# First tile's attention scores one level later in the inverse, and the first retrieval head's scores directly behind their query

## The chip, the cores and the metric

The kernel runs on one core of one Trainium2 chip. The metric is device time in microseconds (us), median of several executions. The engines are TensorE (PE; PEld is its weight load), VectorE (DVE), ScalarE (ACT), GpSimd (POOL) and SyncE (SP, which here only issues DMAs). Each engine runs its own instructions in the order they are written; the engines meet only through semaphores.

## What is computed

One residual block on 1024 tokens of width 1024. A token mixer joins gated DeltaNet (4 heads) and a sliding-window attention with sinks (8 heads); then a product-key retrieval picks 16 of 16384 experts in each of 8 heads, whose outputs are summed. Cut to what matters here:

```python
# DeltaNet, by chunks of 64 tokens: a unit lower triangular system per head
sol = lax.linalg.triangular_solve(a_mat, rhs, left_side=True, lower=True, unit_diagonal=True)
# sliding-window attention
s = jnp.einsum('bnqhgd,bnkhd->bnhgqk', qc, kb) * D ** -0.5
m = jnp.maximum(jnp.max(s, -1, keepdims=True), sink)
p = jnp.exp(s - m)
p = p / (jnp.sum(p, -1, keepdims=True) + jnp.exp(sink - m))
# retrieval
q = (xt @ wq).astype(f32).reshape(n_tok, PEER_HEADS, 2, PEER_HALF)
s1 = jnp.einsum('thd,hnd->thn', q[:, :, 0], k1.astype(f32))
s2 = jnp.einsum('thd,hnd->thn', q[:, :, 1], k2.astype(f32))
t1, i1 = lax.top_k(s1, PEER_TOPK)
t2, i2 = lax.top_k(s2, PEER_TOPK)
h = jnp.einsum('td,ted->te', xb.astype(f32), u[eb].astype(f32))   # experts' hidden values
```

## The kernel before

The program is a row of stages. `project` (to about 285 us) makes the projections. `mix_tokens` then goes through 8 tiles of 128 tokens, one after another; tile 0 takes from about 285 to 344 us. `retrieve` (about 665 to 1000 us) makes queries, scores and searches for 8 heads, and `build_gates` and `experts` follow behind a barrier. The order on every engine is written out by hand in the functions `body` (one copy per engine, run once per tile) and in the lists at the end of `tensor`, `scalar` and `vector` of `retrieve`.

**Tile 0.** The triangular inverse is found in a loop over n from 0 to 5 (`LV` is 6), whose passes are called levels here; levels 0 to 4 do the same thing in turn, level 5 a shorter form of it. At each level PE multiplies (L783), DVE masks the product (L1084, into `m_xc`), PE multiplies twice more (L804, L814), and DVE adds the results (L1093, L1101, into `m_tu`). In between, DVE carries other work: the scores of half the attention heads are scaled and masked (`softmax_scores`, L1045), their row maximum is taken (`softmax_max`, L1053 to L1058), ACT takes the exponentials (`exps`, L908 and L911), DVE sums and inverts (`softmax_sum`, L1064 and L1066), and ACT scales the probabilities (`scale_probs`, L916). DVE's `ahead` (L1013 to L1032) prepares the next tile; its step 1 (L1018) reads `m_rowB`, which a DMA brings. Only in tile 0, the output weights `w_out` are also split into two parts: SP loads them in 8 pieces into two buffers (L649), ACT rounds a piece (`split_wout`, L930), and DVE forms the remainder (`split_wout`, L1070). These lines tie the three together:

```python
            for k in range(KC):                    # SP, sync()
                if k >= 2:
                    sp.wait_ge(wout_lo, k - 1)
                sp.dma_start(wout_raw[k % 2][:], io["w_out"][k * P:(k + 1) * P, :]).then_inc(wout_in[k % 2], 16)
```

So piece k is loaded when DVE has done piece k - 2. ACT's order in tile 0 is: `exps` of the first half, piece 0, two exponentials for the next tile, `scale_probs`, pieces 1 and 2, probabilities out of PSUM, pieces 3 and 4, `exps` of the second half, pieces 5, 6 and 7, and then the copy of `uu` (L953), for which PE waits at L838. DVE does piece n - 1 at the end of level n, piece 5 behind the levels, pieces 6 and 7 later.

The tile's data come by five DMAs on SP in the order queries, keys (`m_kw`), values, gates and mask (`m_wm`); their semaphores are `tile_in[0][0]` to `tile_in[0][4]`. The keys and values of the DeltaNet for tile 0 came earlier with another semaphore. Before the change, PE waits for `tile_in[0][0]` ahead of its first transposes (L759, L761), and DVE waits for `tile_in[0][4]` ahead of everything in the tile.

**Retrieval, head 0.** The head's two queries (`query(0, 0)` and `query(0, 1)`, L1313 to L1315) are made in two halves of 512 tokens, the second of which is 24 matmuls 128x512. ACT copies each half out of PSUM (`query_half`, L1442), PE makes the scores (`score_half`, L1353), ACT copies these (`scores_half`, L1447), and DVE searches them (`search`, L1500 on). PE also makes the hidden values of a block of experts (`hidden(0, 0)` and `hidden(0, 1)`, L1326 to L1328, 12 matmuls each). Before the change each half of `hidden` stands between a query and its score. Head 1's queries follow, without a half of `hidden` between them. ACT copies head 1's queries, rounds weights (`weights`, L1392), and rounds the expert block (`split_u`, L1397); DVE waits for that at its own `split_u` (L1494), halfway through its work on head 0.

## Time and profile before

| | us |
|---|---|
| median of 3 runs | 3067.59 |
| lowest and highest | 3065.72, 3067.85 |
| profiled execution | 3062.79 |
| its span | 3061.1 |
| outside the span | 1.7 |

Shares of the span: PE 85%, PEld 66%, DVE 75%, ACT 34%, POOL 53%. The timeline gives an instruction's start and its length, and in brackets how long the engine sat idle before it and what ended the wait. An engine's next instruction can start slightly ahead of the end of the one before, since they overlap in its pipeline; distances from start to start are therefore used for work in a row.

### The profile page before, as it was taken

How to read it: one execution, taken by the hardware profiler on the slowest of the kernel's cores; microseconds unless marked ns; L12 is line 12 of the kernel's file. 1: busy time of each engine (PE TensorE's matmuls, PEld its weight loads, DVE VectorE, ACT ScalarE, POOL GpSimd, SP SyncE). 2: the span in 40 equal slices, each digit the busy share in tenths (PEclk: the TensorE clock that was granted, in tenths of full speed). 3: DMA queues.
4: the chain of work that ended last, by engine and by line, in shares of the span. 5: the costliest groups of instructions: out<-in, count | busy, mean ns of one | idle time of the engine just before them, and what ended most of it. 6: DMA issues, size and time to landing. Idle time of an engine off the chain costs nothing.

```text
span 3061.1 us, 40460 instructions
## 1 busy us (share of the span) xinstructions
PE 2617.2 (85%) x14808; PEld 2033.3 (66%) x14808; DVE 2307.9 (75%) x4894; ACT 1049.6 (34%) x1649; POOL 1620.0 (53%) x1187
## 2 busy tenths in 40 slices
PE   7998788889996565644678999999999999999996
PEld 5886676778775565542445767777767777677775
DVE  4512667657999899965777778777778777789999
ACT  4412334333544676751112222322222322222322
POOL 0010011024887555545666666677666767766774
PEclk9999899999998787876889999999999999999999
DMA  4323222131111799999999999999999999999995
GB/s 129 127 81 118 85 87 87 45 119 52 58 59 36 260 300 309 322 296 373 379 383 387 391 386 382 401 394 397 387 394 376 408 404 409 391 382 347 366 377 209
DMA packets 309808, 833.44 MB, mean 272 GB/s; under 512 B 26128, under 2 KB 114640, under 8 KB 309616
## 3 DMA queue, kind: packets, MB, share of 16 engines
q0 software_dynamic: 150864, 548.60, 46.7%
q1 hardware_dynamic: 158752, 282.31, 26.1%
q8 instruction: 116, 1.90, 0.3%
q14 instruction: 76, 0.62, 0.1%
HBM read 771.93 MB, written 58.88 MB: 271 GB/s over the span
## 4 chain that ended last, share of the span: by engine, by line
PE 18%; DVE 12%; DMA 12%; POOL 8%; issue 5%; ACT 0%; SPq 0%; DVEq 0%; ACTq 0%; POOLq 0%
DMA e_u_row<-in_u,ids 11%; POOL hold L2081 5%; DVE e_u_row L2319 3%; PE psum L2157 3%; PE psum L2124 3%; PE psum L2158 3%; PE psum L2159 3%; PE psum L2125 3%; PE psum L2126 2%; PE psum L2172 2%; POOL e_u_row L2072 2%; DVE e_y L2309 2%; DVE e_u_row L2328 1%; DVE e_vl L2277 1%; DVE hold L2328 1%
## 5 line engine op out<-in xcount | busy, mean ns | idle before, releaser
L2072 POOL DMA_INDIRECT e_u_row<-in_u,ids x384 | 485.6, 1265 | 330.3 <-DVE ids L2319 236.3
L2319 DVE CUSTOM_DVE_ANT_0 e_u_row<-e_u_row,hold 128x1024 f32<-128x1024 f32 x384 | 468.3, 1224 | 242.6 <-DMA e_u_row<-in_u,ids 242.0
L2157 PE MATMUL psum<-e_vh,e_ah 128*128 128x512 f32 x1024 | 420.7, 411 | 102.1 <-DVE e_y L2309 82.6
L2081 POOL DMA_INDIRECT hold<-in_v,ids x376 | 435.5, 1158 | 134.4 <-issue 108.8
L2158 PE MATMUL psum<-e_vl,e_ah 128*128 128x512 f32 x1024 | 409.2, 400 | 0.0
L2159 PE MATMUL psum<-e_vh,e_al 128*128 128x512 f32 x1024 | 407.4, 398 | 0.0
L2124 PE MATMUL psum<-x1d,e_uh 128*128 128x512 f32 x864 | 341.0, 395 | 0.0
L2125 PE MATMUL psum<-x1d,e_uh 128*128 128x512 f32 x864 | 337.2, 390 | 0.0
L2157 PEld LDWEIGHTS psum<-e_vh,e_ah 128*128 128x128 f32 x1024 | 198.1, 193 | 209.2 <-DVE e_y L2309 109.9
L2126 PE MATMUL psum<-x1d,e_ul 128*128 128x512 f32 x864 | 336.3, 389 | 0.0
L2309 DVE TENSOR_TENSOR e_y<-e_y,psum 128x512 f32<-128x512 f32 x464 | 299.7, 681 | 13.1 <-PE psum L2159 13.1
L1751 PE MATMUL psum<-g_one,g_two 128*128 128x128 f32 x1024 | 172.8, 348 | 130.5 <-DVE g_one L1804 130.5
L1822 POOL DMA_INDIRECT hold<-in_u,ids x128 | 191.4, 1496 | 167.1 <-DVE ids L1783 132.1
L1751 PEld LDWEIGHTS psum<-g_one,g_two 128*128 128x128 f32 x1024 | 167.7, 261 | 143.3 <-issue 143.3
L2217 ACT ACTIVATE e_a<-psum 128x512 f32<-128x512 f32 x108 | 64.3, 596 | 573.4 <-PE psum L2126 573.3
L2206 ACT ACTIVATE e_vh<-e_vr 128x1024 fp32r<-128x1024 f32 x128 | 135.4, 1058 | 339.5 <-DMA e_vr<-in_v 339.2
L2159 PEld LDWEIGHTS psum<-e_vh,e_al 128*128 128x128 f32 x1024 | 197.7, 193 | 44.0
L2158 PEld LDWEIGHTS psum<-e_vl,e_ah 128*128 128x128 f32 x1024 | 198.4, 194 | 39.0
L2172 PE MATMUL psum<-hold,e_column 128*32 128x512 f32 x1536 | 190.4, 615 | 31.4 <-ACT e_column L2223 24.2
L2124 PEld LDWEIGHTS psum<-x1d,e_uh 128*128 128x128 f32 x864 | 162.1, 188 | 64.3 <-issue 31.0
L1178 POOL TENSOR_TENSOR hold<-hold,m_lng 128x1024 f32<-128x1024 f32 x8 | 18.9, 2363 | 346.8 <-DVE hold L1001 346.8
L2212 ACT ACTIVATE e_ah<-e_a 128x512 fp32r<-128x512 f32 x128 | 81.0, 632 | 316.1 <-DVE e_a L2289 316.1
(407 smaller groups left out, 5628.9 us busy)
## 6 DMA issues: line engine op xcount, KB each, us to landing
e_vr<-in_v SPq DMA_DIRECT2D x128, 512.0 KB, 6.7
e_ur<-in_uT SPq DMA_DIRECT2D x108, 512.0 KB, 7.2
s_G<-g_tile SPq DMA_DIRECT2D x8, 4096.0 KB, 27.0
e_g<-s_G SPq DMA_DIRECT2D x64, 512.0 KB, 9.0
ids<-in_w_ch SPq DMA_DIRECT2D x17, 512.0 KB, 4.1
s_ch<-p_out POOLq DMA_DIRECT2D x16, 512.0 KB, 3.3
hold<-in_wq SPq DMA_DIRECT2D x16, 512.0 KB, 4.4
hold<-in_v,ids POOLq DMA_INDIRECT x476, 8.7
```

The lines of the kernel that those rows point to most:

```text
L1751: last = nc.tensor.matmul(psum[:, n // 4, (n % 4) * NK:(n % 4 + 1) * NK], one2[s][:, n, :], one1[s][:, n, :], start=True, stop=True)
L2072: pool.indirect_dma_start(out=u_ring[n % U_RING][:], out_offset=None, in_=io["u"], in_offset=bass.IndirectOffsetOnAxis(ap=id_u[:, s, k:k + ...
L2081: pool.indirect_dma_start(out=v_ring[m % V_RING], out_offset=None, in_=io["v"], in_offset=bass.IndirectOffsetOnAxis(ap=id_v[:, t:t + 1], a ...
L2124: nc.tensor.matmul(psum[:, j, :], uh[j][:, k, :], x1d[0][:, k, :], start=(k == 0), stop=False)
L2125: nc.tensor.matmul(psum[:, j, :], uh[j][:, k, :], x1d[1][:, k, :], start=False, stop=False)
L2126: last = nc.tensor.matmul(psum[:, j, :], ul[j][:, k, :], x1d[0][:, k, :], start=False, stop=(k == KC - 1))
L2157: nc.tensor.matmul(acc, ah[s][j][:, r], vh[s][j][:, c], start=(first and j == 0), stop=False)
L2158: nc.tensor.matmul(acc, ah[s][j][:, r], vl[s][j][:, c], start=False, stop=False)
L2159: last = nc.tensor.matmul(acc, al[s][j][:, r], vh[s][j][:, c], start=False, stop=(final and j == 1))
L2172: last = nc.tensor.matmul(psum[32 * j:32 * j + 32, 6 + c, :], column[:, 32 * (4 * (n % Z_RING) + j) + 31 - i:32 * (4 * (n % Z_RING) + j) + ...
L2309: add = nc.vector.tensor_tensor(y[:, t, c], y[:, t, c], psum[:, bank(g, q), :], ALU.add)
L2319: nc.vector.tensor_tensor_reduce(row, row, xs[:, s, :], 1.0, 0.0, ALU.mult, ALU.add, hs[:, s, k:k + 1]).then_inc(dotted, 1)
```

## The change

In tile 0 only (`before` is false there), PE no longer waits for the queries' load ahead of its transposes. The first half's attention scores (`scores(s, 0)` on PE) come behind the multiply of level 1 with their own wait for queries and keys. On DVE, `softmax_scores` and `softmax_max` of that half come at the end of level 1, and `softmax_sum` at the end of level 2 in place of level 1. DVE's wait for the mask stands behind the two products `kd` and `vb` and ahead of level 0. ACT's order in tile 0 is the same. Tiles 1 to 7 keep their order. In head 0 of the retrieval, each `score_half` of the second token half directly follows its query, and both halves of `hidden` follow the second score; on ACT, `scores_half(0, 1)` goes ahead of the first weights of head 1.

```diff
--- before.py
+++ after.py
@@ -754,17 +754,17 @@
             def body(c, i, s, before, after):
                 now = c + 1
 
-                pe.wait_ge(tile_in[s][0], 16 * (i + 1))
+                if before:
+                    pe.wait_ge(tile_in[s][0], 16 * (i + 1))
                 for h in range(GH):
                     nc.tensor.transpose(bank(2)[:, h, :], ch[s][:, GH + h, :], ident)
                 for h in range(GH):
                     last = nc.tensor.transpose(bank(3)[:, h, :], ch[s][:, 2 * GH + h, :], ident)
                 last.then_inc(S["tr"], 1)
-                pe.wait_ge(tile_in[s][1], 16 * (i + 1))
                 if before:
+                    pe.wait_ge(tile_in[s][1], 16 * (i + 1))
                     pe.wait_ge(S["ma_lo"], c)
-                scores(s, 0)
-                if before:
+                    scores(s, 0)
                     pe.wait_ge(S["mg_lo"], c)
                     pe.wait_ge(wout_lo, KC)
                     pe.wait_ge(S["h1"], 2 * (c - 1))
@@ -785,6 +785,10 @@
                     last.then_inc(lx, 1)
                     if before:
                         project_out(1 - s, sum(share[:n]), share[n])
+                    if n == 1 and not before:
+                        for part in range(2):
+                            pe.wait_ge(tile_in[s][part], 16 * (i + 1))
+                        scores(s, 0)
                     if n == 3:
                         pe.wait_ge(S["p_nrm"], 2 * c + 1)
                         transpose_probs(0)
@@ -1072,11 +1076,12 @@
 
             def body(c, i, s, before, after):
                 now = c + 1
-                dve.wait_ge(tile_in[s][4], 16 * (i + 1))
                 dve.wait_ge(S["tr"], now)
                 nc.vector.tensor_tensor(kd[:], bank(2), per_head("kdec", c), ALU.mult)
                 nc.vector.tensor_tensor(vb[:], bank(3), per_head("beta", c), ALU.mult).then_inc(S["kd"], 1)
-                softmax_scores(c, s, 0)
+                dve.wait_ge(tile_in[s][4], 16 * (i + 1))
+                if before:
+                    softmax_scores(c, s, 0)
                 for n in range(LV):
                     dve.wait_ge(lx, c * LV + n + 1)
                     if n < LV - 1:
@@ -1105,13 +1110,15 @@
                         last.then_inc(lb, 1)
                     else:
                         nc.vector.tensor_copy(full_u[blocks[0], :, blocks[1]], half_bank(3)[blocks[0]]).then_inc(lb, 1)
-                    if n == 0:
+                    if n == 1 and not before:
+                        softmax_scores(c, s, 0)
+                    if n == (0 if before else 1):
                         softmax_max(c, 0)
                     if n == 4:
                         softmax_scores(c, s, 1)
                     if after and n in (0, 1, 2, 4):
                         ahead(c + 1, i + s, 1 - s, {0: 1, 1: 2, 2: 4, 4: 5}[n])
-                    if n == 1:
+                    if n == (1 if before else 2):
                         softmax_sum(c, 0)
                     if not before and n:
                         split_wout(n - 1)
@@ -1368,11 +1375,11 @@
             score_half(1, 0)
             pe.wait_ge(mixer.x_lo, NT)
             query(0, 0, (1,))
-            hidden(0, 0)
             score_half(0, 1)
             query(0, 1, (1,))
-            hidden(0, 1)
             score_half(1, 1)
+            for part in range(2):
+                hidden(0, part)
             for h in range(1, PH):
                 query(h, 0)
                 query(h, 1)
@@ -1458,8 +1465,8 @@
             mixer.x1_high(act, 7)
             scores_half(1, 0)
             query_half(0, 1)
+            scores_half(0, 1)
             weights(1, (0,))
-            scores_half(0, 1)
             query_half(1, 1)
             scores_half(1, 1)
             weights(1, (1,))
```

DVE in tile 0, from level 1's mask. In the kernel before (`m_xc` is the masked product, `m_tu` the two running sums, `m_mx` the softmax's row values, `x1d<-hold,x1s` is a piece of `w_out`):

```order
L1084 TENSOR_TENSOR m_xc<-psum,mats 128x256
L1093 TENSOR_TENSOR m_tu<-m_tu,psum 128x256
L1101 TENSOR_TENSOR m_tu<-m_tu,psum 128x256
L1020 TENSOR_TENSOR hold<-m_rowB,hold 128x512
L1064 TENSOR_TENSOR m_mx<-m_mx 128x4
L1066 RECIPROCAL m_mx<-m_mx 128x4
L1070 TENSOR_TENSOR x1d<-hold,x1s 128x1024
L1084 TENSOR_TENSOR m_xc<-psum,mats 128x256
L1025 TENSOR_TENSOR m_qd<-m_ch,hold 128x512
```

With the change (line numbers are 4 or 5 higher):

```order
L1089 TENSOR_TENSOR m_xc<-psum,mats 128x256
L1098 TENSOR_TENSOR m_tu<-m_tu,psum 128x256
L1106 TENSOR_TENSOR m_tu<-m_tu,psum 128x256
L1049 SCALAR_TENSOR_TENSOR hold<-psum,m_wm 128x1024
L1057 TENSOR_REDUCE m_mx<-hold 128x4
L1059 TENSOR_TENSOR m_mx<-m_mx,sinks 128x4
L1061 TENSOR_TENSOR m_mx<-sinks,m_mx 128x4
L1062 TENSOR_SCALAR m_mx<-m_mx 128x4
L1024 TENSOR_TENSOR hold<-m_rowB,hold 128x512
L1074 TENSOR_TENSOR x1d<-hold,x1s 128x1024
L1089 TENSOR_TENSOR m_xc<-psum,mats 128x256
L1029 TENSOR_TENSOR m_qd<-m_ch,hold 128x512
```

The mask of the scores, the maximum and its three small operations moved from level 0 to behind level 1, ahead of the first piece of `w_out`; the sum and the reciprocal moved out, to the next level:

```order
L1098 TENSOR_TENSOR m_tu<-m_tu,psum 128x256
L1106 TENSOR_TENSOR m_tu<-m_tu,psum 128x256
L1033 TENSOR_TENSOR m_aq<-psum,hold 128x512
L1068 TENSOR_TENSOR m_mx<-m_mx 128x4
L1070 RECIPROCAL m_mx<-m_mx 128x4
L1074 TENSOR_TENSOR x1d<-hold,x1s 128x1024
```

There the sum and the reciprocal now stand directly ahead of the second piece of `w_out`.

PE in the retrieval's head 0, at the end of the second half of the first query, before:

```order
L1314 MATMUL psum<-x1d,w 128x512
L1315 MATMUL psum<-x1d,w 128x512
L1326 MATMUL psum<-x1d,r_uh 128x512
L1327 MATMUL psum<-x1d,r_uh 128x512
L1328 MATMUL psum<-x1d,r_ul 128x512
```

and with the change:

```order
L1321 MATMUL psum<-x1d,w 128x512
L1322 MATMUL psum<-x1d,w 128x512
L1360 MATMUL psum<-r_kk,hold 128x128 x4
L1320 MATMUL psum<-x1d,r_wh 128x512
L1321 MATMUL psum<-x1d,r_wh 128x512
```

The scores (`r_kk`) moved up to the query; 12 matmuls of `hidden` went from here to behind the second score.

ACT there, before:

```order
L1442 ACTIVATE hold<-psum 128x512
L1392 ACTIVATE w<-hold 128x1024
L1447 ACTIVATE r_sc<-psum 128x512
L1442 ACTIVATE hold<-psum 128x512
L1447 ACTIVATE r_sc<-psum 128x512
```

and with the change:

```order
L1449 ACTIVATE hold<-psum 128x512
L1454 ACTIVATE r_sc<-psum 128x512
L1399 ACTIVATE w<-hold 128x1024
L1449 ACTIVATE hold<-psum 128x512
L1454 ACTIVATE r_sc<-psum 128x512
```

The copy of the scores (`r_sc`) moved ahead of the rounding of the weights.

## Rows read from the trace of the kernel before

**Rows 1.** The page's first line: span and instructions of the whole execution.
```profile
span 3061.1 us, 40460 instructions
```

**Rows 2.** Timeline of DVE, tile 0: start, length, instruction, [idle before <-releaser].
```profile
293.66 0.69 DVE L1077 TENSOR_TENSOR m_kd<-psum,d_kdec 128x512 f32<-128x512 f32 x1 [9.09 <-DMA m_wm<-in_wmask]
...
294.87 1.22 DVE L1045 SCALAR_TENSOR_TENSOR hold<-psum,m_wm 128x1024 f32<-128x1024 f32 x1
...
296.00 0.41 DVE L1084 TENSOR_TENSOR m_xc<-psum,mats 128x256 f32<-128x256 f32 x1
...
298.00 1.21 DVE L1053 TENSOR_REDUCE m_mx<-hold 128x4 f32<-128x1024 f32 x1
...
300.76 0.69 DVE L1018 TENSOR_TENSOR hold<-m_rowB,hold 128x512 f32<-128x512 f32 x1 [1.07 <-DMA m_rowB<-s_rows]
```

**Rows 3.** Timeline of DVE, tile 0, inverse levels 1 to 3 and later.
```profile
303.86 0.42 DVE L1101 TENSOR_TENSOR m_tu<-m_tu,psum 128x256 f32<-128x256 f32 x1 [0.43 <-PE psum L814]
...
304.80 0.16 DVE L1064 TENSOR_TENSOR m_mx<-m_mx 128x4 f32<-128x4 f32 x1
...
306.20 0.42 DVE L1084 TENSOR_TENSOR m_xc<-psum,mats 128x256 f32<-128x256 f32 x1
...
308.80 1.22 DVE L1070 TENSOR_TENSOR x1d<-hold,x1s 128x1024 fp32r<-128x1024 f32 x1
...
309.94 0.42 DVE L1084 TENSOR_TENSOR m_xc<-psum,mats 128x256 f32<-128x256 f32 x1
...
325.30 1.20 DVE L1070 TENSOR_TENSOR x1d<-hold,x1s 128x1024 fp32r<-128x1024 f32 x1
```

**Rows 4.** Timeline of ACT, tile 0, same columns.
```profile
299.72 0.51 ACT L908 ACTIVATE hold<-hold,m_mx 128x256 f32<-128x256 f32 x1 [13.98 <-DVE m_mx L1058]
...
301.70 0.19 ACT L911 ACTIVATE m_mx<-m_mx 128x4 f32<-128x4 f32 x1
...
305.88 1.69 ACT L916 ACTIVATE hold<-hold,m_mx 128x256 f32<-128x256 f32 x4
...
331.73 1.06 ACT L930 ACTIVATE x1s<-hold 128x1024 fp32r<-128x1024 f32 x1 [2.53 <-DMA hold<-in_w_out]
...
332.70 0.58 ACT L953 ACTIVATE m_uu<-psum 128x512 f32<-128x512 f32 x1
```

**Rows 5.** DMA issues, 255 to 345 us: count, KB, median us to landing.
```profile
hold<-in_w_out SPq DMA_DIRECT2D x8, 512.0 KB, 4.0
```

**Rows 6.** Timeline of PE, tile 0, same columns.
```profile
301.84 1.12 PE L804 MATMUL psum<-m_xc,m_tu 64*64 64x64 f32 x16 [3.49 <-DVE m_xc L1084]
...
306.67 0.68 PE L804 MATMUL psum<-m_xc,m_tu 64*64 64x64 f32 x16 [0.73 <-DVE m_xc L1084]
...
333.33 2.08 PE L838 MATMUL psum<-m_uu,m_kd 128*128 128x128 f32 x8 [5.05 <-ACT m_uu L953]
```

**Rows 7.** Timeline of PE, retrieval's head 0.
```profile
694.46 0.39 PE L1326 MATMUL psum<-x1d,r_uh 128*128 128x512 f32 x1
...
697.18 1.05 PE L1353 MATMUL psum<-r_kk,hold 128*128 128x128 f32 x8
...
707.05 0.48 PE L1313 MATMUL psum<-x1s,w 128*128 128x512 f32 x1
```

**Rows 8.** Timeline of ACT, retrieval's heads 0 and 1.
```profile
694.66 0.60 ACT L1442 ACTIVATE hold<-psum 128x512 f32<-128x512 f32 x1 [6.54 <-PE psum L1315]
...
731.93 1.04 ACT L1397 ACTIVATE r_uh<-r_ur 128x1024 fp32r<-128x1024 f32 x1
```

**Rows 9.** Timeline of DVE, retrieval's heads 0 and 1.
```profile
699.01 0.87 DVE L1500 MAX8 r_top<-r_sc 128x8 f32<-128x128 f32 x4 [5.00 <-ACT r_sc L1447]
...
708.07 0.87 DVE L1500 MAX8 r_top<-r_sc 128x8 f32<-128x128 f32 x4 [3.80 <-ACT r_sc L1447]
...
733.00 1.60 DVE L1494 TENSOR_TENSOR r_ul<-r_ur,r_uh 128x1024 fp32r<-128x1024 f32 x1 [7.43 <-ACT r_uh L1397]
```

**Rows 10.** Windows, 734 to 1000 us: busy PE, PEld, DVE, ACT, POOL; PEclk, DMA, GB/s.
```profile
734.00:1000.00 266.00, 225.94 (x1035) 187.51 (x1033) 253.68 (x1504) 127.45 (x108) 211.38 (x96) 0.92 0.16 51
```

## Prediction, made before the changed kernel ran

> **What bounds the kernel now.** I read three views: the timelines of the first tile engine by engine, the timelines around the retrieval's head 0, and one window over the rest of the retrieval. The shares of the page don't help, since the two edited places are 60 us and 40 us of a span of 3061.1 us [rows 1], each with a limit of its own. The stages follow each other with nothing to fill a gap, so I carry a delay of either place to the end in full.
>
> Tile 0 begins with DVE idle until the mask lands at 293.66, and later it stands still once more until `m_rowB` lands at 300.76 [rows 2]. Its end is set by ACT: the copy of `uu` at 332.70 is queued behind the last piece of `w_out`, which ACT could start only when it had landed at 331.73 [rows 4], and PE waited 5.05 us for `uu` [rows 6]. That last piece was sent for when DVE had done piece 5, begun at 325.30 and ended at 326.50 [rows 3], so it took 5.2 us to land, where the median of the eight is 4.0 [rows 5]. The path through tile 0 is thus DVE's row of levels and pieces, one load, and ACT.
>
> In head 0 of the retrieval DVE idles 5.00 and 3.80 us for scores, and then 7.43 us for ACT's rounding of an expert block [rows 9]. ACT does that at 731.93 [rows 8], behind the copies of head 1's queries, which PE makes from 707.05 on without a pause [rows 7]. From 734 to 1000 us DVE is busy 253.68 of 266 us [rows 10], so whatever moves the end of the third idle time moves the rest.
>
> **Start of tile 0: nothing on the path.** PE's transposes and DVE's two products go ahead of the load, and DVE's level 0 starts at 293.7, when the mask is there, instead of 296.00 [rows 2]: 2.3 us earlier. But the next-tile step with `m_rowB` still stands between level 0 and level 1, and its landing doesn't depend on DVE: SP sends for it before the first `w_out`. It starts at 300.76 as before; the idle time grows from 1.07 us by the 2.3 us and by the maximum, which is no longer there. The scores on PE lie in that hole too.
>
> **Levels 1 and 2: +5.3 us.** DVE's last addition of level 1 starts at 303.86 as before [rows 3] and the next instruction about 0.35 later, at 304.2. Now come the scores (294.87 to 296.00, 1.13 us [rows 2]): 305.3. The maximum and its small ones, which begin when the scores are written, take 1.7 us to ACT's start (298.00 to 299.72 [rows 2, 4]): 307.1. ACT's exponentials take 299.72 to 301.70 and 0.19 [rows 4], 2.2 us: 309.3. Only behind these stands ACT's piece 0 (1.06 us [rows 4]): 310.3. DVE has one small step to do meanwhile and then waits for it; its piece 0 takes 1.14 us from start to start (308.80 to 309.94 [rows 3]). Level 2 starts at 311.5 instead of 306.20. Before, the exponentials ran while DVE waited for `m_rowB`; that cover is gone.
>
> **Level 2 to level 3: +3.1 us more.** Before, DVE went from level 2's start to piece 1 in 2.60 us and finished it in 1.14 [rows 3], together 3.74, because ACT had long rounded that piece. Now the sum and the reciprocal come first (0.3 us; the sum alone is the 0.16 us row of [rows 3]), then ACT scales the probabilities (four in about 1.6 us [rows 4]), then rounds piece 1 (1.06), each handing over in some 0.05 us, and only then does DVE do its piece: 2.60 + 0.3 + 1.6 + 1.06 + 0.1 + 1.14 = 6.8. That is 3.1 more, and level 3 starts 8.4 us later than before. From there DVE has the same list as before, ACT's pieces are ahead of it, and each load follows DVE's pieces; at the median 4.0 us the loads keep up. So piece 5, the last load and `uu` are 8.4 us later.
>
> **PE's clock: +2.6 us.** After an idle time of 3.49 us the sixteen small matmuls of a level took 1.12 us, and after one of 0.73 us only 0.68 [rows 6]: 0.44 us more for L804, and the same again for L814 behind it, 0.88 us a level. That is the engine at 1.2 instead of 2.4 GHz. With the change PE stands idle about 6 us ahead of level 2 and some 2 us more twice until level 3. I charge levels 2, 3 and 4, 2.6 us, as that row after 3.49 us is the nearest; the ends are 0 (the clock stays up) and 3.5 (four levels).
>
> Tile 0 is then 5.3 + 3.1 + 2.6 = 11.0 us longer, with bounds 8.4 - 1.2 = 7.2 (the clock stays up and the last load takes 4.0 instead of 5.2) and 8.4 + 3.5 = 11.9.
>
> **Retrieval, head 0: +1.7 us.** Between a query and its score must lie ACT's copy. The query ended at 694.46, where `hidden` began; ACT started 0.20 later [rows 7, 8], and PE starts 0.63 us after ACT's start, as with `uu` (332.70 to 333.33 [rows 4, 6]). Before, 2.72 us of `hidden` (694.46 to 697.18 [rows 7]) covered that. Now PE idles 0.83 us twice, and as the same matmuls have to be done, head 1's queries start at 708.7 instead of 707.05: 1.7 us. For DVE the two searches start earlier, at 699.01 - (2.72 - 0.83) = 697.1, and at 708.07 - 3.8 = 704.3: here two halves of `hidden` are gone, 5.4 us, and two gaps have come, 1.7. But its next wait, until 733.00 [rows 9], ends with ACT's rounding of the block behind head 1's queries. It only grows from 7.43 to 7.4 + 3.8 + 1.7 = 12.9 us and ends at 734.7. ACT's and POOL's rounding of head 1's weights come later by one copy of scores, about 1.7 us, and were finished well ahead of their use. The bounds are 0 (a gap is covered somehow) and 1.7, since a gap of 0.83 us is about the 0.73 us which left the clock up in [rows 6].
>
> **Sum.** 11.0 + 1.7 = 12.7 us. The profiled execution took 3062.79 us, 1.7 outside its span, and would be 3075.5. The median of the runs is 3067.59, 4.8 above it; the same 12.7 us on it give 3080.3, and I forecast 3080.
>
> **The rivals.**
> *The slack in front of `uu` hides part of tile 0.* PE waits 5.05 us for `uu` [rows 6], so DVE's row of levels has about that much slack if the last loads don't depend on it. Then tile 0 costs 11.0 - 5.05 = 6.0, and the time is 3067.6 + 6.0 + 1.7 = 3075.3. Against it: the loads wait for DVE's pieces by the code quoted above, and all pieces shift. Chance 0.08.
>
> *The retrieval's gain gets through.* DVE is the busiest engine from 734 us on, and its search starts 3.8 us earlier. If the 7.43 us of [rows 9] ended by the DMA of the block rather than by PE's queries, DVE would keep the 3.8: 3067.6 + 11.0 - 3.8 = 3074.8. The Trainium skill (Perfetto Trace Analysis, Identifying Performance Opportunities) says to take the most contended engine of a stretch and to make what its gaps wait for start sooner, which is what this edit does for DVE; by that rule it is a gain. The row says the gap behind is the one that decides, with ACT idle until PE's queries. Chance 0.09.
>
> *Faster.* Both at once, at one point: if DVE doesn't fall behind the loads of `w_out` by more than the 5.05 us in front of `uu`, tile 0 costs nothing, and the search's 3.8 us remain: 3063.8. It decides at the second piece: were ACT to have it rounded before `scale_probs`, level 3 would be only 5.3 us late. ACT's order speaks against it. Chance 0.07.
>
> *The forecast,* with tile 0 between 7.2 and 11.9 and the retrieval between 0 and 1.7, that is 3074.8 to 3081.2 and on either side some 2 us by which the medians of different runs stand apart: chance 0.76, its own range 3073 to 3083.
>
> **How the numbers follow.** The range that holds the time 8 times in 10 runs from 3070 to 3085: the forecast's, and both partly hidden cases. A measurement of this kernel can tell about 0.2%, 6.1 us, from no change, so slower begins at 3073.7. The faster rival gives 0.07. Of the two partly hidden cases (0.17) more than half, and of the forecast's low end a little, fall below 3073.7 once the runs' own spread is added: 0.14 for no change. Slower is left with 0.79.
>
> **What would show it.** In tile 0: DVE idle some 5 us until `m_rowB`, still at about 300.8; idle about 2.5 us ahead of piece 0 and nearly 3 ahead of piece 1, both ended by ACT L930's counterpart; level 2 at 311.5; `uu` at about 344; L804's counterpart at 1.12 us in levels 2 and 3. In the retrieval, seen relative to the tile's shift: two gaps of 0.8 us on PE in front of the scores, head 1's queries 1.7 us later, DVE's wait for the block 12.9 us. I am wrong if `m_rowB` lands earlier, if DVE finds piece 0 or 1 ready, or if the stages behind take up a shift.

## The result: slower by 0.4%

| | before | after |
|---|---|---|
| median of 10 runs each | 3063.56 us | 3072.95 us |
| lowest and highest | 3057.98, 3067.85 | 3069.38, 3077.55 |
| profiled execution | 3062.79 | 3069.38 |
| its span | 3061.1 | 3067.7 |

The ratio is 1.0039, with a 95% interval of 1.0029 to 1.0050: slower by 0.4%, 11.9 us by the ratio and 9.4 by the medians. The forecast was 3080.0 with a range of 3070 to 3085. The ratio is not the quotient of the two medians, which is 1.0031. The lines of the changed kernel are numbered 4, 5 or 7 higher in the places shown.

**Tile 0.** First DVE's timeline of the changed kernel: start in us, length, engine and line, operation, output and inputs, and in brackets the idle time before it and what ended that.

```profile
294.07 0.42 DVE L1089 TENSOR_TENSOR m_xc<-psum,mats 128x256 f32<-128x256 f32 x1 [5.90 <-DMA m_wm<-in_wmask]
...
301.34 0.69 DVE L1022 TENSOR_TENSOR hold<-m_rowB,hold 128x512 f32<-128x512 f32 x1 [4.35 <-DMA m_rowB<-s_rows]
...
304.78 1.22 DVE L1049 SCALAR_TENSOR_TENSOR hold<-psum,m_wm 128x1024 f32<-128x1024 f32 x1
...
310.90 1.23 DVE L1074 TENSOR_TENSOR x1d<-hold,x1s 128x1024 fp32r<-128x1024 f32 x1 [2.59 <-ACT x1s L934]
312.04 0.42 DVE L1089 TENSOR_TENSOR m_xc<-psum,mats 128x256 f32<-128x256 f32 x1
...
318.56 1.23 DVE L1074 TENSOR_TENSOR x1d<-hold,x1s 128x1024 fp32r<-128x1024 f32 x1 [2.72 <-ACT x1s L934]
319.70 0.42 DVE L1089 TENSOR_TENSOR m_xc<-psum,mats 128x256 f32<-128x256 f32 x1
...
323.67 0.42 DVE L1089 TENSOR_TENSOR m_xc<-psum,mats 128x256 f32<-128x256 f32 x1
327.37 0.42 DVE L1098 TENSOR_TENSOR m_tu<-m_tu,psum 128x256 f32<-128x256 f32 x1 [3.29 <-PE psum L808]
...
337.56 1.19 DVE L1074 TENSOR_TENSOR x1d<-hold,x1s 128x1024 fp32r<-128x1024 f32 x1
```

Four idle times behind the start stand out. DVE is through with level 0 early and stands 4.35 us until `m_rowB` is there (1.07 us in [rows 2]). It stands 2.59 and 2.72 us for ACT's pieces 0 and 1, where it had no wait before, and it stands 3.29 us in level 4 for PE, where it was 1.61 us before. The level starts (L1089) are at 294.07, 301.95, 312.04, 319.70 and 323.67. ACT's timeline shows where pieces 0 and 1 come from:

```profile
307.75 0.51 ACT L912 ACTIVATE hold<-hold,m_mx 128x256 f32<-128x256 f32 x1 [21.56 <-DVE m_mx L1062]
...
309.83 1.04 ACT L934 ACTIVATE x1s<-hold 128x1024 fp32r<-128x1024 f32 x1
...
315.88 1.70 ACT L920 ACTIVATE hold<-hold,m_mx 128x256 f32<-128x256 f32 x4 [3.54 <-DVE m_mx L1070]
317.48 1.99 ACT L934 ACTIVATE x1s<-hold 128x1024 fp32r<-128x1024 f32 x2
...
342.57 1.06 ACT L934 ACTIVATE x1s<-hold 128x1024 fp32r<-128x1024 f32 x1 [1.69 <-DMA hold<-in_w_out]
343.53 0.58 ACT L957 ACTIVATE m_uu<-psum 128x512 f32<-128x512 f32 x1
```

ACT has done nothing for 21.56 us when the row maximum comes at 307.75. Its exponentials run until 309.7, and only behind them comes piece 0 (309.83). Piece 1 (317.48) stands behind `scale_probs` (315.88), which had to wait for DVE's reciprocal. In [rows 4] the exponentials began at 299.72, at a time when DVE was waiting for a DMA anyway. At the end the last piece (342.57) and `uu` (343.53) follow each other as in [rows 4]. PE's timeline:

```profile
294.55 1.12 PE L808 MATMUL psum<-m_xc,m_tu 64*64 64x64 f32 x16 [7.16 <-DVE m_xc L1089]
...
302.42 1.12 PE L808 MATMUL psum<-m_xc,m_tu 64*64 64x64 f32 x16 [3.19 <-DVE m_xc L1089]
...
312.51 1.12 PE L808 MATMUL psum<-m_xc,m_tu 64*64 64x64 f32 x16 [5.91 <-DVE m_xc L1089]
...
320.17 1.12 PE L808 MATMUL psum<-m_xc,m_tu 64*64 64x64 f32 x16 [1.45 <-DVE m_xc L1089]
...
322.93 2.08 PE L723 MATMUL psum<-m_kw,hold 64*128 64x256 f32 x8
...
326.64 0.68 PE L808 MATMUL psum<-m_xc,m_tu 64*64 64x64 f32 x16
...
344.16 2.07 PE L842 MATMUL psum<-m_uu,m_kd 128*128 128x128 f32 x8 [3.62 <-ACT m_uu L957]
```

L808, the counterpart of L804 in [rows 6], takes 1.12 us in levels 0 to 3 and 0.68 us in level 4. The second half's scores (L723) take 2.08 us, just behind 1.12 us ones. The longer times are PE at the lower of its two clock levels. Level 1 had 1.12 us before the change too [rows 6]; what is new is the low clock in levels 0, 2 and 3 and in the matmuls of level 4 ahead of L808. Windows of 4 us show the clock for both kernels (us, then busy us and instruction count of PE, PEld, DVE, ACT and POOL, then the granted clock as a share of 2.4 GHz, the DMA share and GB/s). Before:

```profile
304.00:308.00 4.00, 3.21 (x58) 2.76 (x56) 3.73 (x9) 3.28 (x7) 0.00 (x0) 0.87 0.18 25
308.00:312.00 4.00, 3.12 (x68) 2.68 (x70) 3.17 (x7) 2.48 (x3) 0.00 (x0) 1.00 0.54 143
312.00:316.00 4.00, 3.94 (x66) 3.24 (x62) 2.33 (x5) 1.06 (x1) 0.00 (x0) 1.00 0.58 224
...
320.00:324.00 4.00, 3.04 (x16) 2.63 (x16) 3.90 (x8) 2.37 (x10) 0.00 (x0) 0.50 0.44 139
```

and after:

```profile
304.00:308.00 4.00, 2.61 (x32) 2.30 (x28) 3.47 (x8) 0.24 (x1) 0.00 (x0) 0.78 0.01 5
308.00:312.00 4.00, 0.00 (x0) 0.00 (x0) 1.41 (x2) 4.00 (x12) 0.00 (x0) 0.65 0.00 0
312.00:316.00 4.00, 2.83 (x48) 2.64 (x48) 2.75 (x8) 0.46 (x2) 0.00 (x0) 0.50 0.35 131
...
320.00:324.00 4.00, 3.83 (x54) 3.54 (x56) 2.35 (x5) 0.91 (x2) 0.00 (x0) 0.50 0.36 131
```

From 308 to 316, levels 3 and 4 of the kernel before, the clock was 1.00; after, PE does nothing from 308 to 312, and then has 0.50, that is 1.2 GHz. Before had its own stretch at 0.50, but later, from 320 on.

To compare the stages I count from the first DVE instruction of the tile's preparation (`m_xc`, 283.69 before, 284.14 after, which is t0 below), as the stages ahead differ by 0.45 us.

| after t0, us | level 0 | 1 | 2 | 3 | 4 | `uu` |
|---|---|---|---|---|---|---|
| before | 12.31 | 17.68 | 22.51 | 26.25 | 29.39 | 49.01 |
| after | 9.93 | 17.81 | 27.90 | 35.56 | 39.53 | 59.39 |
| difference | -2.38 | +0.13 | +5.39 | +9.31 | +10.14 | +10.38 |

**Retrieval, head 0.** PE's timeline of the changed kernel:

```profile
701.77 0.39 PE L1322 MATMUL psum<-x1d,w 128*128 128x512 f32 x1
702.85 1.16 PE L1360 MATMUL psum<-r_kk,hold 128*128 128x128 f32 x8 [0.69 <-ACT hold L1449]
703.76 0.48 PE L1320 MATMUL psum<-x1d,r_wh 128*128 128x512 f32 x1
...
710.14 1.16 PE L1360 MATMUL psum<-r_kk,hold 128*128 128x128 f32 x8 [0.69 <-ACT hold L1449]
```

and DVE's, whose third row is the forming of the expert block's remainder (L1501):

```profile
704.78 0.88 DVE L1507 MAX8 r_top<-r_sc 128x8 f32<-128x128 f32 x4 [3.24 <-ACT r_sc L1454]
...
712.08 0.88 DVE L1507 MAX8 r_top<-r_sc 128x8 f32<-128x128 f32 x4 [2.02 <-ACT r_sc L1454]
...
742.45 1.61 DVE L1501 TENSOR_TENSOR r_ul<-r_ur,r_uh 128x1024 fp32r<-128x1024 f32 x1 [12.87 <-ACT r_uh L1404]
```

DVE waits 3.24 and 2.02 us for the scores where [rows 9] have 5.00 and 3.80, so the searches do start sooner. PE stands 0.69 us ahead of each score for ACT's copy of the query, where the matmul in the third row starts without a wait. And DVE's next wait, for ACT's rounding of the expert block (L1404), has grown from 7.43 us [rows 9] to 12.87. From tile 7's last layer norm to the end of that wait it is 63.41 us before and 65.31 after: 1.90 us more.

**Where the profiled execution's 6.6 us lie.** +0.45 ahead of t0, +10.38 in tile 0, -1.84 in tiles 1 to 7, -1.44 from there to the layer norm, +1.90 in head 0, +0.36 in the rest of the retrieval, and -3.21 in the gates and experts. The change reaches none of the negative places. Most of the -1.84 and the -1.44 is two stretches in which the kernel before had a low clock and the changed one did not, as the windows show. Before:

```profile
490.00:494.00 4.00, 4.00 (x25) 3.23 (x23) 1.44 (x5) 2.65 (x5) 0.00 (x0) 0.66 0.02 4
650.00:654.00 4.00, 4.00 (x11) 3.19 (x12) 0.00 (x0) 1.04 (x2) 3.92 (x3) 0.60 0.00 0
```

and after:

```profile
500.00:504.00 4.00, 3.94 (x58) 3.34 (x56) 2.30 (x7) 2.66 (x5) 0.00 (x0) 1.00 0.02 4
659.00:663.00 4.00, 4.00 (x17) 3.26 (x18) 0.00 (x0) 1.05 (x2) 3.92 (x3) 1.00 0.00 0
```

These are the same places of the same tiles, and PE is busy 3.94 to 4.00 of 4 us in all of them. The last term is the gates and experts, unchanged in every kernel here: 2058.1 us before and 2054.9 after in the profiles, and from 2051.5 to 2060.9 over the twelve profiles of this study. A run's time therefore scatters by several us whatever is done elsewhere (how the 9.4 us come about was not looked into), and the experiments below are read by stage as well as by their ratios.

### The profile page after: what moved, and what is told of

The parts are those of the page before. It is cut to its first block, busy times and chain, and to the rows that moved or that the text cites. A ratio compares the mean times of both kernels' runs of the same rounds, so it can differ in the third digit from the quotient of the medians.

```text
span 3067.7 us, 40461 instructions
## 1 busy us (share of the span) xinstructions
PE 2615.0 (85%) x14808; PEld 2031.9 (66%) x14808; DVE 2307.7 (75%) x4894; ACT 1048.1 (34%) x1649; POOL 1601.2 (52%) x1187
## 4 chain that ended last, share of the span: by engine, by line
PE 14%; DMA 13%; DVE 13%; POOL 9%; issue 6%; ACT 0%; DVEq 0%; SPq 0%; ACTq 0%; POOLq 0%
DMA e_u_row<-in_u,ids 12%; POOL hold L2088 6%; DVE e_u_row L2326 3%; POOL e_u_row L2079 3%; PE psum L2164 2%; PE psum L2131 2%; PE psum L2165 2%; PE psum L2166 2%; PE psum L2132 2%; PE psum L2133 2%; DVE e_y L2316 2%; PE psum L2179 2%; DVE e_u_row L2335 2%; DVE e_vl L2284 1%; DVE hold L2335 1%
## 5 line engine op out<-in xcount | busy, mean ns | idle before, releaser
L2088 POOL DMA_INDIRECT hold<-in_v,ids x376 | 428.0, 1138 | 130.5 <-issue 109.2
```

The lines of the kernel that those rows point to most:

```text
L2088: pool.indirect_dma_start(out=v_ring[m % V_RING], out_offset=None, in_=io["v"], in_offset=bass.IndirectOffsetOnAxis(ap=id_v[:, t:t + 1], a ...
```

## Experiments

All are timed beside runs of the kernel before on the same chip; the medians of those were 3060.67 us (e1 to e4), 3059.97 (e5 to e8) and 3058.76 (e9, e10). My theory was that tile 0 pays through ACT's order and DVE's waits plus PE's clock, and the retrieval through PE's two gaps; the rivals were that the slack ahead of `uu` hides part of it, and that DVE keeps its earlier search. Each kernel has one profile, so a stage's time is one sample. Where nothing waits for a DMA and the clock is the same, the samples repeat: levels 1 to 2, 2 to 3 and 3 to 4 take 10.10, 7.65 and 3.97 us in e1 and 10.09, 7.66 and 3.97 in the changed kernel, the same code. The loads do not: `uu` comes 49.01, 49.34 and 47.37 us after t0 in the kernel before, e2 and e7, which have the same tile 0.

### e1: the change in tile 0 alone

The changed kernel with the retrieval's order put back.

```diff
             query(0, 0, (1,))
+            hidden(0, 0)
             score_half(0, 1)
             query(0, 1, (1,))
+            hidden(0, 1)
             score_half(1, 1)
-            for part in range(2):
-                hidden(0, part)
...
+            weights(1, (0,))
             scores_half(0, 1)
-            weights(1, (0,))
```

> The change with the retrieval's part undone. My theory (nearly all of the loss is in tile 0, where ACT's exponentials and scaling now stand uncovered in front of the pieces of w_out, with PE at 1.2 GHz on top): the copy of uu 10 to 11 us later than in the kernel before, tiles 1 to 7 and the retrieval unchanged but for that shift, and 3 to 4 us of it lost or not by chance in single stretches where PE's clock drops; time 10 us over the kernel before. Rival (the first tile's loss is made up by slack in the later stages, and the retrieval is what costs): time within 3 us of the kernel before.

Measured: 3070.61 us, ratio 1.0053 [1.0037, 1.0069]. Levels 2, 3 and 4 start 27.10, 34.76 and 38.72 us after t0 and `uu` 58.15, 9.1 later than before. From the layer norm to the end of the wait for the block's rounding it is as long as before (63.44 us). So tile 0 alone makes nearly all of the loss, and no slack hides it. The run times fit that but say little on the size: the six runs give 16 us by the ratio and 9.9 by the medians, which lies below the ratio's own interval (11 to 21 us). Tile 0 lost 9.1 us to `uu` here and 10.4 in the changed kernel, with the same instructions. Of the 1.2 us, 0.8 is `m_rowB`, which let level 1 start at 17.00; from there to level 4 the steps are equal. In level 4 DVE waited 2.44 us for PE here and 3.29 there, and the last load took 0.4 us more here.

### e2: the change in the retrieval alone

The kernel before with the same lines of `tensor` and `scalar` in `retrieve` in the changed order.

```diff
             query_half(0, 1)
-            weights(1, (0,))
-            scores_half(0, 1)
+            scores_half(0, 1)
+            weights(1, (0,))
             query_half(1, 1)
```

> Only the retrieval's part of the change on the kernel before. My theory (head 1's queries decide): two gaps of 0.8 us on PE ahead of the scores, DVE's wait for the rounded expert block about 13 us instead of 7.4, and the rest of the retrieval 1.7 to 1.9 us later; time 1.7 us over the kernel before. Rival (DVE, the busiest engine there, keeps what its searches gain): DVE's work behind that wait starts 3.8 us earlier, time 3.8 us under the kernel before.

Measured: 3061.37 us, 1.0009 [0.9997, 1.0021]. PE's timeline:

```profile
694.47 1.16 PE L1353 MATMUL psum<-r_kk,hold 128*128 128x128 f32 x8 [0.69 <-ACT hold L1442]
...
701.77 1.16 PE L1353 MATMUL psum<-r_kk,hold 128*128 128x128 f32 x8 [0.69 <-ACT hold L1442]
```

and DVE's:

```profile
734.08 1.61 DVE L1494 TENSOR_TENSOR r_ul<-r_ur,r_uh 128x1024 fp32r<-128x1024 f32 x1 [12.87 <-ACT r_uh L1397]
```

The gaps of 0.69 us and the wait of 12.87 us are those of the changed kernel; from the layer norm to here it is 65.33 us where it was 63.41. The ratio can't tell +1.9 us from nothing, but it excludes the 3.8 us of gain of the second rival (0.9988), and the stage shows a loss. The Trainium skill (Perfetto Trace Analysis, Identifying Performance Opportunities) has one shorten the gaps of the most contended engine. Here two gaps of that engine were shortened, from 5.00 and 3.80 us [rows 9] to 3.23 and 2.03, and the sum with the third grew from 16.23 to 18.13 us all the same, because the third is ended by ACT behind PE's queries.

### e3: ACT rounds pieces 0 and 1 first

The changed kernel, with two pieces moved in ACT's order of tile 0.

```diff
-                exps(c, 0)
                 if not before:
                     split_wout(0)
+                exps(c, 0)
                 if after:
                     decays_ahead(act, c + 1, i + s, 1 - s)
-                scale_probs(c, 0)
                 if not before:
                     split_wout(1)
+                scale_probs(c, 0)
+                if not before:
                     split_wout(2)
```

> The changed kernel with two moves on ACT in tile 0: piece 0 of w_out is rounded ahead of the exponentials and piece 1 ahead of the scaling of the probabilities. DVE's order is as in the changed kernel. My theory (DVE's waits for pieces 0 and 1, 2.59 and 2.72 us in the changed kernel, are ACT's work put in front of them): both waits go, level 3 starts 5.3 us earlier than in the changed kernel, and as PE then idles less, up to 1 us more; time 5 to 6 us under the changed kernel, 6 us over the kernel before. Rival (the waits are for the loads of w_out): both waits stay, time as the changed kernel's.

Measured: 3069.25 us, 1.0030 [1.0016, 1.0044]. Both of DVE's waits are gone and level 3 starts at 30.28, 5.3 us earlier than in the changed kernel. At `uu` 4.5 of it are left (54.86). The run times show less than the 5 to 6 us under the changed kernel that I expected: by the ratios the two kernels are 0.1% apart, and the intervals overlap. Level 3 takes 6.16 us here for 3.97. PE waits there for the probabilities. In the changed kernel it did so as well,

```profile
317.63 1.09 PE L730 MATMUL psum<-cst,hold 128*128 128x128 f32 x8 [2.29 <-ACT hold L920]
```

but DVE was standing for piece 1 at the time. Here DVE has done piece 1 and level 3's mask, the matmuls behind the wait take 1.97 us for 1.09,

```profile
315.74 1.97 PE L730 MATMUL psum<-cst,hold 128*128 128x128 f32 x8 [2.28 <-ACT hold L920]
```

and DVE waits for what PE does behind them:

```profile
318.80 0.42 DVE L1099 TENSOR_TENSOR m_tu<-m_tu,psum 128x256 f32<-128x256 f32 x1 [3.42 <-PE psum L808]
```

So the order on ACT is one cause of the loss, but with the pieces ahead PE's wait for the probabilities, covered until then, is on the path.

### e4: filler on PE

The changed kernel with 48 more 128x128 matmuls on PE in tile 0, into a bank that nobody reads, in four groups (12, 22, 9 and 5) where PE stood idle. They add work and change no result.

```diff
                         scores(s, 0)
+                        fill(12)
...
+                    if n == 2 and not before:
+                        fill(22)
...
+                        if not before:
+                            fill(9)
                         pe.wait_ge(S["p_nrm"], 2 * c + 1)
                         transpose_probs(0)
+                        if not before:
+                            fill(5)
```

> The changed kernel with 48 further 128x128 float32 matmuls on PE in tile 0, written to a PSUM bank that nothing reads then, in its idle times of levels 1, 2 and 3; they add work and change no result. My theory (in levels 1 to 4 PE runs at 1.2 GHz since it idles, which costs 2.5 us or more): the sixteen small matmuls of a level take 0.68 us instead of 1.12 in levels 2 and 3, uu is 2 to 3 us earlier than in the changed kernel, time 2 to 3 us under it. Rival (the clock has no part in the loss, or the added work costs as much as it gives): time as the changed kernel's or over it.

Measured: 3063.6 us, 1.0021 [1.0006, 1.0036], with more work than the changed kernel. The windows of 4 us:

```profile
304.00:308.00 4.00, 4.00 (x39) 4.00 (x38) 2.25 (x6) 2.21 (x10) 0.00 (x0) 1.00 0.01 4
308.00:312.00 4.00, 2.56 (x51) 2.23 (x51) 2.83 (x5) 2.38 (x3) 0.00 (x0) 1.00 0.19 39
...
320.00:324.00 4.00, 3.18 (x52) 2.52 (x48) 2.30 (x6) 1.28 (x2) 0.00 (x0) 1.00 0.46 142
```

and PE's timeline:

```profile
310.55 0.68 PE L819 MATMUL psum<-m_xc,m_tu 64*64 64x64 f32 x16 [1.39 <-DVE m_xc L1100]
...
317.39 0.68 PE L819 MATMUL psum<-m_xc,m_tu 64*64 64x64 f32 x16 [0.33 <-DVE m_xc L1100]
...
319.21 1.13 PE L723 MATMUL psum<-m_kw,hold 64*128 64x256 f32 x8
```

The clock stays at 1.00 from 300 to 324. The small matmuls of levels 1 to 3 take 0.68 us instead of 1.12 (level 0's still take 1.12), and the second half's L723 takes 1.13 instead of 2.08. DVE's two waits for ACT are the same 2.59 and 2.72 us. Levels 2, 3 and 4 start at 26.52, 33.36 and 36.50 and `uu` at 54.72. Taken step by step, levels 1 to 2, 2 to 3, 3 to 4 and 4 to `uu` are 0.82, 0.82, 0.83 and 1.64 us shorter than in the changed kernel, 4.1 us in all. Level 1 comes 0.56 earlier, which is within what `m_rowB`'s landing varies (17.00 in e1). The first 0.82 is no part of the change's loss, since level 1 ran at the low clock in the kernel before as well (1.12 us [rows 6]). That leaves 3.3 us for the change, where the prediction had 2.6. The clock is thus a cause of its own, separate from the waits. That it is the clock and nothing else of the filler is shown by the durations: the same instructions, 1.12 and 0.68 us, at 0.50 and 1.00 granted.

### e5: `m_rowB` ahead of the tile's loads

The changed kernel, with `load_rows(sp, 1, 1)` moved ahead of the waits and of tile 0's loads on SP.

```diff
             load_x(sp, 1, 1)
+            load_rows(sp, 1, 1)
             sp.wait_ge(front.stored[1], 16 * (N_CH // 2))
             sp.wait_ge(front.stored[0], 16 * (N_CH // 2 + 1))
             load(sp, 0, 0, first=N_CONV)
             load(sp, 1, 1)
-            load_rows(sp, 1, 1)
```

> The changed kernel with the load of m_rowB for tile 1 sent for ahead of tile 0's other loads instead of behind tile 1's. My theory (level 1 can't start before m_rowB is there, so nothing at the start of the tile was to be had): DVE's 4.35 us of idle time in front of it go, level 1 starts about 4.9 us earlier, and all of it reaches uu; time 4 to 5 us under the changed kernel. Rival (a later wait, for the loads of w_out or for tile 1's data, takes its place): less than 2 us under it.

Measured: 3068.88 us, 1.0029 [1.0018, 1.0041]. DVE no longer waits for `m_rowB`; level 1 starts at 12.77 instead of 17.81, 5.0 us sooner, and `uu` at 55.23, 4.2 sooner. So the hole until `m_rowB` really held the start of the softmax back. Piece 5 even starts 5.9 us sooner, and what is missing at `uu` is the last load, which took 5.6 us from the end of piece 5 where it took 3.8. The run times don't separate it from the changed kernel; the stage does.

### e6: tile 0 in another order

The retrieval as before. In tile 0, `m_rowB` and the first two pieces are loaded ahead, the mask is awaited only at the scores, the scores come at the end of level 1 on DVE and behind level 2's multiply on PE, DVE does a piece at every level from 0 on, and ACT rounds pieces 0 and 1 ahead of the exponentials.

```diff
-                exps(c, 0)
-                if not before:
+                if before:
+                    exps(c, 0)
+                    decays_ahead(act, c + 1, i + s, 1 - s) if after else None
+                else:
                     split_wout(0)
-                if after:
+                    split_wout(1)
                     decays_ahead(act, c + 1, i + s, 1 - s)
+                    exps(c, 0)
+                    split_wout(2)
                 scale_probs(c, 0)
...
-                    if not before and n:
-                        split_wout(n - 1)
+                    if not before:
+                        split_wout(n)
```

> Tile 0 ordered anew, the retrieval as in the kernel before: m_rowB and the first two pieces of w_out are sent for first, DVE waits for the mask only ahead of the scores, these come behind level 1 and piece 1, ACT rounds pieces 0 and 1 and makes tile 1's exponentials ahead of the first softmax, and DVE does piece n in level n instead of n - 1. My theory (the hole until 300.8 us can be filled with levels 0 and 1 and two pieces if nothing in front waits for a load): level 2 starts at about 298 us instead of 306.2, uu at about 323 instead of 332.7; time 9 us under the kernel before. Rival (tile 1's 1 MB load and the later pieces of w_out, which then share the DMA engines with it, take the place of the waits): less than 3 us under it.

Measured: 3052.25 us, 0.9977 [0.9963, 0.9991]. `uu` is at 44.47 after t0, 4.5 sooner than before and 14.9 sooner than in the changed kernel. With loads that scatter by 2 us the first of these numbers is rough. I had expected it at 323 us and it came at 328.72. Two waits stand in the way that the changed kernel doesn't have. PE's is for `m_ch`, the 1 MB of data of tile 1:

```profile
299.12 2.08 PE L692 MATMUL psum<-m_ch 128*128 128x128 f32 x8 [2.60 <-DMA m_ch<-s_ch]
```

`m_ch` landed 14.8 us after t0, and 14.0 in the kernel before: PE comes to it sooner now, and the pieces of `w_out` that are sent for ahead of it can account for 0.9 of the 2.60 us at most. DVE's wait is for piece 5, which ACT rounds behind the exponentials of the second half:

```profile
322.72 1.22 DVE L1077 TENSOR_TENSOR x1d<-hold,x1s 128x1024 fp32r<-128x1024 f32 x1 [2.14 <-ACT x1s L935]
```

### e7: DVE does not stop for the expert block

The kernel before; DVE's `split_u(2, 0)` moves behind head 0's gates, and ACT's `gates(0)` between its copies for head 1.

```diff
-                if more:
+                if more and h:
                     split_u(h + 2, v)
                 dve.wait_ge(sorting, 4 * h + 4)
...
                                         ALU.mult).then_inc(g_out, 1)
+                if h == 0:
+                    split_u(2, 0)
```

> The kernel before with two moves in the retrieval: DVE splits the expert block for head 2 behind the gates of head 0 instead of halfway through its positions, and ACT makes the exponential of head 0's gates between its copies of head 1's two queries. My theory (DVE's 7.43 us in front of the block are set by head 1's queries on PE, while 8 us of its own work stand behind): the search of head 1 starts at about 735 us instead of 742.3, and since DVE is busy 95% of the time from there, time 5 to 7 us under the kernel before. Rival (PE or POOL is next in line and keeps the pace): the search starts earlier, but the retrieval ends within 2 us of where it did.

Measured: 3053.0 us, 0.9978 [0.9964, 0.9991]. Head 1's search starts 65.19 us after the layer norm instead of 72.66, 7.5 us sooner. At the end of the retrieval 4.0 us of that are left (329.44 instead of 333.40 from the layer norm to the gates). 2.2 us of the difference lie in one instruction of DVE,

```profile
765.60 2.39 DVE L1581 TENSOR_SCALAR r_pab<-r_pos 128x128 uint32<-128x128 uint32 x1
```

which runs beside a subtraction on POOL's timeline:

```profile
764.54 3.36 POOL L1642 TENSOR_TENSOR r_wl<-hold,r_wh 128x1024 fp32r<-128x1024 f32 x1
```

In the kernel before the same operation of head 1 took 0.21 us, at 774.79, when POOL had ended. There it was head 0's that met a subtraction and took 2.41 us (0.23 us here), so the slow one has moved from ahead of head 1's search, where it is part of the 7.5 us, to behind it.

### e8: e6 and e7 together

> Both together, tile 0 ordered anew and the two moves in the retrieval. My theory: the gains add, since the stages follow one another: 13 to 16 us under the kernel before. Rival: one of them takes the other's place, not more than 9 us under it.

Measured: 3049.2 us, 0.9957 [0.9942, 0.9973]. The ratio is what 0.23% and 0.22% make together, but its interval (8 to 18 us) doesn't exclude the rival's 9. The stages show both gains: `uu` is at 44.02, and from the layer norm to the gates it is 329.39 us.

### e9: `uu` ahead of pieces 6 and 7

The kernel before, with one move in ACT's order of tile 0.

```diff
                 exps(c, 1)
                 if not before:
                     split_wout(5)
-                    split_wout(6)
-                    split_wout(7)
                 act.wait_ge(S["u_mm"], now)
                 nc.scalar.activation(uu[:], bank(1), ACT.Copy).then_inc(S["u_ev"], 1)
+                if not before:
+                    split_wout(6)
                 scale_probs(c, 1)
+                if not before:
+                    split_wout(7)
```

> The kernel before with ACT's copy of uu in tile 0 moved ahead of its pieces 6 and 7 of w_out, the scaling of the second half's probabilities between these. My theory (the end of tile 0 is set by one queue order: uu stands behind a piece whose load DVE's own pieces send for): uu 5 us earlier, at about 327.5 us, PE's wait for it under 1 us instead of 5.05, and pieces 6 and 7 in time for tile 1; time 4 to 5 us under the kernel before. Rival (the next tile waits for the pieces instead, as DVE does them before its sum of squares): uu is earlier, tile 1 is not.

Measured: 3052.9 us, 0.9980 [0.9969, 0.9992]. ACT's timeline:

```profile
328.00 0.60 ACT L951 ACTIVATE m_uu<-psum 128x512 f32<-128x512 f32 x1 [2.52 <-PE psum L832]
```

`uu` (328.00) now waits for PE's product and no longer for a load; it comes 43.74 us after t0, 5.3 sooner, and PE doesn't wait for it. Tile 1's `uu` comes 7.1 us sooner than before, so pieces 6 and 7 hold nothing up there, which was the rival. This is the step with which the prediction ended tile 0: the copy stood in ACT's queue behind a load that it doesn't need.

### e10: e8 with `uu` and piece 5 ahead

ACT's order of the second half is piece 5, `exps(c, 1)`, piece 6, `uu`, `scale_probs(c, 1)`, piece 7.

> The kernel with tile 0 ordered anew and the two moves in the retrieval, and on top ACT's piece 5 ahead of the second softmax's exponentials and its copy of uu ahead of piece 7. My theory (DVE's 2.14 us in front of piece 5 and uu's wait for the last load are ACT's order once more): uu about 4 us earlier than in that kernel; time 14 us or more under the kernel before. Rival (the load of 1 MB for tile 1, for which PE waits 2.6 us in level 2, and PE's clock keep the pace): less than 1 us under that kernel.

Measured: 3043.74 us, 0.9948 [0.9932, 0.9963], faster than both kernels. The run times don't separate it from e8, so the rival (less than 1 us under that kernel) is answered by the stage alone: `uu` is at 40.82 after t0, 3.2 us sooner than in e8, 8.2 than before and 18.6 than in the changed kernel, and PE's product for `uu` is what ACT waits for:

```profile
324.87 0.60 ACT L960 ACTIVATE m_uu<-psum 128x512 f32<-128x512 f32 x1 [2.52 <-PE psum L837]
```

## Why the prediction was right, and where it missed

**The direction and the mechanism held, and the size within 0.7 us a stage, in part by luck.** The chance of 0.79 was on slower by over 0.2%, and it is 0.39% [0.29, 0.50].

**Start of tile 0: right.** Level 0 starts 2.38 us sooner (forecast 2.3), DVE then waits 4.35 us for `m_rowB` (forecast some 5), and level 1 starts at the same place, +0.13. `m_rowB` itself landed 0.6 later than assumed (301.34 for 300.76), of which 0.45 is the later t0. PE ran at the low clock in level 0 as well (1.12 us), but in the hole ahead of `m_rowB`, where it costs nothing.

**Levels 1 and 2: right.** +5.39 us at level 2 for a forecast of 5.3. The wait of 2.59 ahead of piece 0 is the cover that is gone, and it is made of the terms of the sum: maximum, exponentials, piece.

**Level 2 to level 3: right in cause, and part of the clock is in it.** The forecast was 3.1 more, and 3.9 came; 0.8 of it is PE's clock, which stood in a term of its own. e3 shows the cause by undoing it: with ACT's two pieces ahead both waits vanish and level 3 comes 5.3 us sooner.

**PE's clock: 3.3 us for 2.6.** The step took 0.88 us for each of levels 2, 3 and 4, from the small matmuls alone. Levels 2 and 3 cost 0.82 and 0.83 (e4). Level 4 cost 1.64 us, and by other matmuls than the step had: L808 was back at 0.68 us there, but the second half's scores ahead of it ran at the low clock (L723, 2.08 us against 1.13 in e4), and DVE's wait for PE in level 4 grew from 1.61 to 3.29 us, which the prediction did not have. With it piece 5 started 11.81 us later than before, where the sum had 11.0. That size is itself one sample: how far into level 4 the low clock lasts differs, and the wait was 2.44 us in e1, which has the same code there.

**The last load: a single sample taken for the rule.** The prediction kept the 5.2 us from piece 5 to the last piece's landing. After, it was 3.8 us (338.75, the end of piece 5, to 342.57). The change has no part in that: with tile 0 as before it was 5.0 us in e2 and 3.7 in e7. Tile 0 was therefore 10.38 us longer instead of 11.0 by two errors of opposite sign, and that it came so near is partly luck: with a last load of the same length on both sides it would have been 11.8.

**Retrieval: right.** Two gaps of 0.69 us (forecast 0.83), DVE's wait 12.87 us (forecast 12.9), head 0 longer by 1.90 us (forecast 1.7). The working is seen best from start to start: the last matmul of the query and the score lie 1.08 us apart (701.77, 702.85), where two matmuls in a row lie 0.23 apart, and the score's own step takes 0.91 us instead of 0.81. That is 0.85 and 0.10, twice. The gap was sized right, and only the 0.10 were not in the sum; the trace's 0.69 us of idle time is counted from a modelled end.

**The sum and the base.** 10.38 + 1.90 is 12.3 us, and the prediction had 12.7. The ratio gives 11.9 us (its interval 8.9 to 15.3) and the medians 9.4. That 3080.0 was 7.05 above the measured 3072.95 comes for the larger part from the base: the median of three runs, 3067.59, was 4.03 above the 3063.56 that ten runs gave. The other 3.0 are 12.7 against the medians' 9.4, less the rounding down of 0.3, and are within the scatter of the gates and experts. The weakest step is the last one, the sum set on a median of three runs, 4.8 above the profiled execution: the same 12.7 us on that execution, 3075.5, stood beside it in the text and was the nearer number. Within that sum the terms that were off are the clock in level 4 and the last load, as said above.

**The rivals.** The slack ahead of `uu` hid nothing (e1: 9.1 us at `uu` from tile 0 alone), since the loads follow DVE's pieces. The retrieval's gain did not get through (e2). Neither did both.

## To carry to other kernels

When work is moved from under a DMA wait to behind it, ask what else was covered there: here it was ACT's exponentials, and what queued behind them in ACT's order was on the path of the other engines. A wait at the head of an in-order queue is worth looking at from the other side as well: moving `uu` ahead of two copies that wait for loads brought 5 us in one edit (e9). And an engine's gap is only worth shortening if its next gap doesn't take the time back (e2), in which case that next gap is the one to remove (e7).

## What the hardware showed that I had not expected

- **The clock was worth 3.3 us of the 10.** Matmuls that are on the path took 1.6 to 1.8 times as long behind stretches in which PE stood idle: the granted clock was 0.50 in 312 to 316 us, after 5.91 us of idle time, and the sixteen 64x64 matmuls took 1.12 us for 0.68. Filler matmuls held it at 1.00 and paid for themselves (e4): `uu` came 4.7 us sooner than in the changed kernel. The Trainium skill (TensorE: Matmul & The Clock Gate, Part 1) puts the penalty of getting up to speed at under 1% of a typical kernel's span. 3.3 us is 0.11% of this one, so that agrees, and yet it is over a quarter of what the change costs.
- **The clock can be low in a busy stretch of one execution and not of another**: with PE busy 4.00 of 4 us, 0.66 and 0.60 were granted in the kernel before, and 1.00 in the same two places after. By the shifts of what follows, each was worth about 1.5 us. PE had stood idle ahead of both stretches in both kernels alike (2.40 and 2.39 us ahead of the first, 1.46 us ahead of the second). From tile 7's `uu` to its layer norm, where the second one lies, it was 28.85 us in six of the twelve profiles, 30.2 to 30.3 in four and 31.6 in two.
- **One small DVE operation took ten times as long beside POOL's subtraction**: 2.39 us instead of 0.21 (e7), and 2.41 us in the kernel before at 734.53 us, again beside a subtraction of the same line. Both times it ended 0.09 us after the subtraction did, as if it had waited for it, and the subtraction took 3.36 and 3.37 us, where most others of its line take 2.4. The cause was not tried.
- **The unchanged stage of gates and experts spread over 9.4 us** in twelve profiles (2051.5 to 2060.9), about the size of the whole effect.
